# Two tables of sums for even and odd experts in the scatter of a mixture of experts

## The chip, the cores and the metric

One core of a Trainium2 chip. The metric is the time of one execution on the device, in microseconds (us). TensorE does the matmuls, VectorE and ScalarE the elementwise work, GpSimd (POOL in the profile) issues the indirect DMAs, SyncE (SP) the direct ones. All DMAs of the core run on its 16 DMA engines.

## The reference

An encoder layer for 1024 tokens of width 1024, in float32: a diagonal state space model and an attention beside each other, a projection with residual and layer norm, then a mixture of experts with a second layer norm. Only the last part matters here:

```python
scores = sigmoid(x1 @ w_router)                 # 64 experts
choice = scores + router_bias                   # top 4 of 8 groups, then top 6 experts
top_w  = top_w / top_w.sum() * 2.5              # weights of the 6 experts of a token
for each block of 128 tokens of one expert e:   # xb: [128, 1024]
    hb = silu(xb @ we_gate[e]) * (xb @ we_up[e])            # [128, 256]
    routed[tok] += (hb @ we_down[e]) * w[:, None]           # scatter with add
shared = (silu(x1 @ ws_gate) * (x1 @ ws_up)) @ ws_down
out = layer_norm(alpha * x1 + routed + shared)
```

## The kernel before, in words

The program has stages that follow each other: `project`, `attention`, `s5_scan`, `s5_gate`, `mix_norm_route` and `moe_experts`. Each has one instruction stream per engine, written out by hand, which wait for each other by semaphores. The change touches the last two.

**`mix_norm_route`** (to line 1388) computes x1 for eight tiles of 128 tokens, routes them, and writes into the DRAM table `slot_d` which token goes to which slot of which expert: VectorE computes the destinations (`route`, `place`), GpSimd scatters (line 1121). SyncE first loads small parameters, waits for `blank_done`, writes blanks over `slot_d` (line 1094), and then stores each finished tile of x1 into `x1_d` (line 1098). At the end the shared expert's gate and up run; ScalarE's `gate(n)` (line 1242) writes `sig` there, a tile of 128 x 1024.

**`moe_experts`** (from line 1391) begins with the shared expert's down product on TensorE (line 1583); VectorE adds alpha times x1 (line 1700), and SyncE stores the eight tiles as the start values of the DRAM table `sum_d` (line 1448). Then 65 blocks follow: one of 128 slots for each of the 64 experts, and one overflow block (more are skipped by tests on `n_over`). For block e:

- GpSimd copies the indices into `idx` (line 1489) and issues four indirect DMAs, a quarter of each row's columns each (line 1493), which gather 128 rows of x1 into `xg[e % 2]`. It waits for `x_turned`, so that the buffer is free.
- VectorE transposes `xg` into `xgT` (line 1678), TensorE computes `p_gu`, gate and up together (line 1547: eight calls of 128x512), ScalarE the sigmoid (line 1615), VectorE the products `gs` and `h` (lines 1683, 1685), TensorE turns h (line 1555), VectorE copies it to `hT`, TensorE computes `p_y` (line 1567, four calls of 128x512).
- ScalarE and VectorE scale one half of `p_y` each into `y[e % 2]` (`keep_y`, lines 1621 and 1695). They wait for the scatter two blocks back, which read the same buffer.
- GpSimd scatters `y` into `sum_d` with an add (line 1504). Before that it waits until the scatter of the block before has landed (line 1502), since two blocks can hold the same token and an add that is in flight reads the old value.

GpSimd's order is gather(e + 4), then scatter(e + 1), and so on; TensorE's is `gate_up(e + 1)`, `down(e)`, `turn_h(e + 1)`. The weights of an expert (three times 1 MB) lie in a ring of four buffers, one of them the tile `o` of the mixers. SyncE loads expert e (lines 1449 to 1454, 1011 and 1015) as soon as block e - 4 has finished its down product; experts 0 to 3 are loaded ahead of the loop, and the overflow block's expert by `load_over(0, 0)`.

When all is scattered, GpSimd has gone through its skipped overflow rounds (lines 1530 to 1535) and has waited for `y_out` (line 1536), SyncE reads the eight tiles of `sum_d` back (line 1476). For each tile t the second layer norm runs: ScalarE adds up the row (line 1663), VectorE makes the mean (`center`, line 1749), ScalarE squares (line 1652), VectorE makes the variance and subtracts the mean (`spread`, lines 1755 and 1756), ScalarE takes the root (line 1657), and VectorE finishes (`finish`, lines 1760 and 1761); SyncE stores the tile (line 1480). VectorE's order is center(t), finish(t - 1), spread(t). TensorE has nothing to do in this part.

## Time and profile before

| | |
|---|---|
| median of three runs | 1798.69 us (1796.7 to 1800.16) |
| profiled execution | 1799.06 us, its span 1797.2 us |
| TensorE matmul busy | 1565.6 us, 87% of the span |
| VectorE / ScalarE / GpSimd busy | 852.0 / 361.7 / 434.0 us |
| DMA | 317.26 MB, 177 GB/s over the span |
| granted TensorE clock, mean | 0.927 |
| expert blocks | first scatter at 1048.7 us, last at 1756.1 us |
| second layer norm | first read of `sum_d` at 1764.14 us |

The page gives busy times of each engine, the chain of work that ended last (followed back from the last instruction, at each step to what released it), the costliest groups of instructions, and for DMAs the time from issue to landing. Times in views are from the start of the span. A matmul call in float32 stands as two instructions. In a group, "idle before" is the time that the engine waited ahead of these instructions, with what ended the wait. Names are without buffer numbers: `sum_d<-moe_y,moe_idx` is the scatter, `moe_xg<-x_d,moe_idx` the gather, `all_x_sb` the tile `k.x`.

### The profile page before, as it was taken

What the parts mean: (1) busy time and instruction counts of PE and PEld (TensorE: products, weight loads), DVE (VectorE), ACT (ScalarE), POOL (GpSimd) and SP (SyncE); (2) the same over time, 40 slices, a digit from 0 to 9 for tenths busy, and PEclk for the clock granted to TensorE, in tenths of its full rate; (3) what the DMA queues carried; (4) which work ended last, traced back from release to release, by engine and by line L of the source; (5) the groups of instructions that cost most, each with busy time, mean ns of one, the idle gap of its engine ahead of it and who ended that gap; (6) DMA issues with size and microseconds to landing.
All of it is one profiled execution on the core that took longest, in us unless ns stands there. A gap on an engine that the chain in (4) does not pass through costs nothing. (4 is left out here: it accounts for less than half of the span.)

```text
span 1797.2 us, 18459 instructions
## 1 busy us (share of the span) xinstructions
PE 1565.6 (87%) x5878; PEld 893.5 (50%) x5878; DVE 852.0 (47%) x1618; ACT 361.7 (20%) x616; POOL 434.0 (24%) x444
## 2 busy tenths in 40 slices
PE   7988999999946555389999999999999999999990
PEld 4545777777735554335554444444444444444440
DVE  1462444444588888324886333333333333333335
ACT  1303444434333113111220010000000000000014
POOL 0000000000000000000234345555555555555530
PEclk9997999999967666689999999999999999999995
DMA  9010000000051101530005679999999999999965
GB/s 233 12 43 4 5 4 4 4 4 1 1 54 17 23 12 23 203 137 24 36 25 203 235 245 368 367 367 361 363 369 369 363 361 368 366 370 366 360 188 204
DMA packets 105149, 317.26 MB, mean 177 GB/s; under 512 B 38358, under 2 KB 55406, under 8 KB 80146
## 3 DMA queue, kind: packets, MB, share of 16 engines
q1 hardware_dynamic: 80546, 257.26, 38.8%
q0 software_dynamic: 23408, 59.45, 13.6%
q8 instruction: 23, 0.38, 0.1%
q10 hardware_dynamic: 1152, 0.00, 0.0%
q14 instruction: 20, 0.16, 0.0%
HBM read 271.73 MB, written 51.72 MB: 180 GB/s over the span
## 5 line engine op out<-in xcount | busy, mean ns | idle before, releaser
L1547 PE MATMUL moe_p_gu<-mixers_ring,moe_xgT 128*128 128x512 f32 x784 | 344.6, 592 | 0.0
L1678 DVE STREAM_TRANSPOSE moe_xgT<-moe_xg 128x1024 f32<-128x1024 f32 x65 | 132.0, 2031 | 423.8 <-DMA moe_xg<-x_d,moe_idx 423.8
L1493 POOL DMA_INDIRECT moe_xg<-x_d,moe_idx x260 | 264.3, 1017 | 116.1 <-issue 60.2
L1121 POOL DMA_INDIRECT slot_d<-all_entry,all_dest_i x48 | 48.1, 1003 | 926.8 <-DVE all_dest_i L1333 914.7
L1567 PE MATMUL moe_p_y<-mixers_ring,moe_hT 128*128 128x512 f32 x520 | 233.9, 592 | 0.9 <-DVE moe_hT L1689 0.9
L1547 PEld LDWEIGHTS moe_p_gu<-mixers_ring,moe_xgT 128*128 128x128 f32 x784 | 145.7, 191 | 164.5 <-issue 164.5
L1504 POOL DMA_INDIRECT sum_d<-moe_y,moe_idx x65 | 105.5, 1623 | 245.3 <-DMA sum_d<-moe_y,moe_idx 209.6
L1567 PEld LDWEIGHTS moe_p_y<-mixers_ring,moe_hT 128*128 128x128 f32 x520 | 98.7, 190 | 125.0 <-issue 123.9
L1615 ACT ACTIVATE moe_sig<-moe_p_gu 128x256 f32<-128x256 f32 x65 | 25.0, 384 | 585.0 <-PE moe_p_gu L1547 585.0
L582 PEld LDWEIGHTS att_p_o<-att_v,att_prT 128*128 128x128 f32 x1024 | 120.4, 192 | 19.5 <-issue 17.6
L582 PE MATMUL att_p_o<-att_v,att_prT 128*128 128x64 f32 x1024 | 123.7, 274 | 1.5 <-DVE att_prT L659 1.5
L529 PE MATMUL att_p_s<-latents_kT,att_qT 96*128 96x512 f32 x256 | 122.3, 601 | 0.0
L645 DVE TENSOR_REDUCE att_nmax<-att_p_s 128x1 f32<-128x1024 f32 x64 | 78.4, 1225 | 92.4 <-PE att_p_s L529 92.1
L1547 PE MATMUL moe_p_gu<-mixers_o,moe_xgT 128*128 128x512 f32 x256 | 113.9, 598 | 1.0
L752 PE MATMUL ssm_p_v<-ssm_U,ssm_w_in 128*128 x256 | 53.1, 397 | 45.3 <-DVE ssm_gsn L859 31.8
L1547 PEld LDWEIGHTS moe_p_gu<-mixers_o,moe_xgT 128*128 128x128 f32 x256 | 47.3, 190 | 57.2 <-issue 57.1
L752 PEld LDWEIGHTS ssm_p_v<-ssm_U,ssm_w_in 128*128 128x128 f32 x256 | 50.3, 303 | 49.5 <-DVE ssm_gsn L859 34.4
L615 ACT ACTIVATE att_pr<-att_p_s,att_bias 128x1024 f32<-128x1024 f32 x64 | 71.0, 1110 | 3.1 <-DVE att_bias L646 3.1
L568 PE MATMUL att_p_t<-all_const,att_pr 128*128 128x128 f32 x512 | 66.9, 274 | 0.9 <-ACT att_pr L615 0.9
L620 ACT ACTIVATE att_prT<-att_p_t 128x512 f32<-128x512 f32 x64 | 38.2, 597 | 138.5 <-PE att_p_t L568 138.5
L1621 ACT ACTIVATE moe_y<-moe_p_y,shared_block_w 128x512 f32<-128x512 f32 x65 | 44.7, 688 | 100.6 <-PE moe_p_y L1567 100.6
L1695 DVE TENSOR_SCALAR moe_y<-moe_p_y,shared_block_w 128x512 f32<-128x512 f32 x65 | 48.7, 749 | 27.7 <-PE moe_p_y L1567 27.1
(314 smaller groups left out, 1966.7 us busy)
## 6 DMA issues: line engine op xcount, KB each, us to landing
mixers_ring<-in_we_down_dram SPq DMA_DIRECT2D x65, 1024.0 KB, 17.3
mixers_ring<-in_we_gate_dram SPq DMA_DIRECT2D x49, 1024.0 KB, 7.7
mixers_ring<-in_we_up_dram SPq DMA_DIRECT2D x49, 1024.0 KB, 14.3
mixers_o<-in_we_gate_dram SPq DMA_DIRECT2D x16, 1024.0 KB, 8.0
mixers_o<-in_we_up_dram SPq DMA_DIRECT2D x16, 1024.0 KB, 14.7
moe_xg<-x_d,moe_idx POOLq DMA_INDIRECT x260, 6.8
all_x_sb<-in_x_dram SPq DMA_DIRECT2D x8, 512.0 KB, 12.3
mixers_ring<-in_w_o_dram SPq DMA_DIRECT2D x1, 4096.0 KB, 22.4
```

What stands on the lines that cost most here:

```text
L529: last = nc.tensor.matmul(p_s[:, t % 2, half * 512:(half + 1) * 512], qT[:, u, t * P:(t + 1) * P], kT[:, u, half * 512:(half + 1) * 512], ...
L568: last = nc.tensor.transpose(p_t[:, j, :], pr[:, t % 2, j * P:(j + 1) * P], k.ident)
L582: last = nc.tensor.matmul(p_o[:, 0:DV], prT[:, t % 2, j, :], v[:, u, j, :], start=(j == 0), stop=(j == T - 1))
L615: nc.scalar.activation(pr[:, t % 2, :], p_s[:, t % 2, :], ACT.Exp, bias=bias[:, t % 2:t % 2 + 1], scale=SCALE, accum_out=total[:, t % 4:t ...
L645: ch.link(nc.vector.tensor_reduce(nmax[:, t % 2:t % 2 + 1], p_s[:, t % 2, :], AX.X, ALU.max, negate=True))
L752: last = nc.tensor.matmul(p_v[:, x % 2, part, r, :], w_in[:, gd, part * N:part * N + P], U[:, bass.ds(b * GB + half * 4 + r, 1), :].rearra ...
L1493: nc.gpsimd.indirect_dma_start(xg[:, u, g, :], None, x1_quarters, bass.IndirectOffsetOnAxis(ap=idx[:, c, g:g + 1], axis=0), bounds_check=N ...
L1504: nc.gpsimd.indirect_dma_start(k.sum_d[:, :], bass.IndirectOffsetOnAxis(ap=idx[:, c, NQ:NQ + 1], axis=0), y[:, u, :], None, compute_op=ALU ...
L1547: last = nc.tensor.matmul(p_gu[:, u, :], xgT[:, u, kk, :], k.moe_gu[v][:, :, kk * F:(kk + 1) * F], start=(kk == 0), stop=(kk == KD - 1))
L1567: last = nc.tensor.matmul(p_y[:, half * 512:(half + 1) * 512], hT[:, u, kk, :], k.moe_dn[v][:, kk * D + half * 512:kk * D + (half + 1) * 512],
L1678: nc.vector.transpose(xgT[:, u].rearrange("p k (g i) -> p g k i", g=NQ), xg[:, u].rearrange("p g (j k) -> p g k j", k=KD)).then_inc(x_turn ...
L1695: nc.vector.tensor_scalar(y[:, u, 512:D], p_y[:, 512:D], k.block_w[:, bass.ds(col, 1)], None, ALU.mult).then_inc(y_dve, 1)
```

## The change

There are two DRAM tables of sums. Even blocks scatter into table 0, odd ones into table 1, and each table has a semaphore `y_out[u]` of its own. A scatter, and `keep_y`, wait for the scatter of the same parity before. Table 0 starts as before; table 1 is set to zero in `mix_norm_route` by one DMA from the tile `sig`, which VectorE wipes first; ScalarE's first `gate` waits for that DMA. At the end SyncE reads both tables, the second one into the ring's `gate_up` buffers 0 and 1, TensorE adds the two tiles by two matmuls with the identity matrix per half into PSUM (`p_sum`, two tiles that take turns), and the layer norm reads PSUM where it read `k.x`. GpSimd's loop has 9 rounds of six blocks instead of 10, the rest is written out; the order of its gathers and scatters is the same.

```diff
-    k.sum_d = nc.dram_tensor("sum_d", (SEQ + P, D), f32).ap()
+    k.sum_d = [nc.dram_tensor(f"sum{u}_d", (SEQ + P, D), f32).ap() for u in range(2)]
...
             sp.wait_ge(blank_done, 1)
+            sp.wait_ge(wiped, 1)
+            sp.dma_start(k.sum_d[1].rearrange("(b p) d -> p b d", p=P),
+                         sig[:, :, :].rearrange("p f t -> p (f t)").unsqueeze(1).to_broadcast([P, T + 1, D])).then_inc(wiped_d, 16)
...
             def gate(n):
                 act.wait_ge(gu_done, n + 1)
+                if n == 0:
+                    act.wait_ge(wiped_d, 16)
...
+            nc.vector.memset(sig[:, :, :], 0.0).then_inc(wiped, 1)
             tokens = k.tok.unsqueeze(2).to_broadcast([P, T, TOP_K])
...
+        part = [k.moe_gu[t // 4].rearrange("p h (a d) -> p (h a) d", d=D)[:, t % 4, :] for t in range(T)]
+        p_sum = [p_y[:, :], p_gu[:, :, :].rearrange("p u w -> p (u w)")]
-        y_out = sem("y_out")
+        y_out = [sem(f"y_out{u}") for u in range(2)]
...
-            sp.wait_ge(all_out, 1)
+            sp.wait_ge(all_out, 2)
             for t in range(T):
-                sp.dma_start(k.x[:, t, :], k.sum_d[t * P:(t + 1) * P, :]).then_inc(sum_in[t], 16)
+                sp.dma_start(k.x[:, t, :], k.sum_d[0][t * P:(t + 1) * P, :]).then_inc(sum_in[t], 16)
+                sp.dma_start(part[t], k.sum_d[1][t * P:(t + 1) * P, :]).then_inc(sum_in[t], 16)
...
-            def scatter(n, u, c, first=False):
+            def scatter(n, u, c, landed):
                 pool.wait_ge(y_act, n + 1)
                 pool.wait_ge(y_dve, n + 1)
-                if not first:
-                    pool.wait_ge(y_out, n * 16)
+                if landed is not None:
+                    pool.wait_ge(y_out[u], landed)
                 pool.sem_inc(y_taken, 1)
-                nc.gpsimd.indirect_dma_start(k.sum_d[:, :], bass.IndirectOffsetOnAxis(ap=idx[:, c, NQ:NQ + 1], axis=0),
-                                             y[:, u, :], None, compute_op=ALU.add).then_inc(y_out, 16)
+                nc.gpsimd.indirect_dma_start(k.sum_d[u], bass.IndirectOffsetOnAxis(ap=idx[:, c, NQ:NQ + 1], axis=0),
+                                             y[:, u, :], None, compute_op=ALU.add).then_inc(y_out[u], 16)
...
-            with pool.Fori(0, (E - 4) // 6) as ee:
+            gather(4, OVER + 4, 0, 4, free=3)
+            scatter(1, 1, 1, None)
+            LOOPED = (E - 5) // 6 * 6
+            with pool.Fori(0, LOOPED // 6) as ee:
                 for v in range(6):
-                    e = ee * 6 + v
-                    gather(e + 4, ee * 6 + (OVER + 4 + v), v % 2, (v + 4) % 6, free=e + 3)
-                    scatter(e + 1, (v + 1) % 2, (v + 1) % 6)
+                    gather(ee * 6 + (v + 5), ee * 6 + (OVER + 5 + v), (v + 1) % 2, (v + 5) % 6, free=ee * 6 + (v + 4))
+                    scatter(ee * 6 + (v + 2), v % 2, (v + 2) % 6, ee * 48 + (v // 2 + 1) * 16)
...
-            pool.wait_ge(y_out, n_over * 16 + 16 * E)
-            pool.sem_inc(all_out, 1)
+            for u in range(2):
+                pool.wait_ge(y_out[u], (n_over + (1 - u)) // 2 * 16 + 8 * E)
+                pool.sem_inc(all_out, 1)
...
+            for t in range(T):
+                pe.wait_ge(sum_in[t], 32)
+                if t >= 2:
+                    pe.wait_ge(squared, t - 1)
+                    pe.wait_ge(centered, t - 1)
+                for half in range(2):
+                    cols = slice(half * 512, (half + 1) * 512)
+                    nc.tensor.matmul(p_sum[t % 2][:, cols], k.ident, k.x[:, t, cols], start=True, stop=False)
+                    last = nc.tensor.matmul(p_sum[t % 2][:, cols], k.ident, part[t][:, cols], start=False, stop=True)
+                last.then_inc(summed, 1)
...
-                act.wait_ge(sum_in[t], 16)
+                act.wait_ge(summed, t + 1)
...
-                nc.scalar.activation(junk[:, :], k.x[:, t, :], ACT.Copy, accum_out=tot[:, 0, t:t + 1]).then_inc(added, 1)
+                nc.scalar.activation(junk[:, :], p_sum[t % 2], ACT.Copy, accum_out=tot[:, 0, t:t + 1]).then_inc(added, 1)
...
-                ch.link(nc.vector.scalar_tensor_tensor(k.x[:, t, :], k.x[:, t, :], nmean[:, t:t + 1], g2[:, :], ALU.add, ALU.mult))
+                nc.vector.scalar_tensor_tensor(k.x[:, t, :], p_sum[t % 2], nmean[:, t:t + 1], g2[:, :], ALU.add, ALU.mult).then_inc(centered, 1)
```

The square reads `p_sum` in the same way, and `keep_y` on both engines waits for `y_out[u]`.

## Rows read from the trace of the kernel before

**Rows 1.** The page, part 4: chain that ended last, shares of the span, by line.
```profile
DMA sum_d<-moe_y,moe_idx 34%; PE moe_p_s L1583 2%; PE moe_p_gu L1547 2%; PE moe_p_y L1567 1%; DVE all_x_sb L1761 1%; DMA moe_xg<-x_d,moe_idx 0%; DVE all_x_sb L1756 0%; DMA all_x_sb<-sum_d 0%; POOLq L1489 0%; POOL moe_xg L1493 0%; POOLq L1530 0%; POOL sum_d L1504 0%; ACT moe_junk L1663 0%; DVE moe_y L1695 0%; ACT L1657 0%
```

**Rows 2.** Line 1504, its instructions: ns min/median/max, first and last start; then its landings.
```profile
L1504 POOL DMA_INDIRECT sum_d<-moe_y,moe_idx x65: 1552/1626/1636, 1048.7 to 1756.1; - x65
...
DMA to landing us min/median/max: 6.3/10.3/11.4
```

**Rows 3.** Stretch 1600 to 1700: busy us of five engines, clock, DMA share, GB/s.
```profile
1600.00:1700.00 100.00, 97.22 (x235) 42.47 (x234) 33.73 (x46) 9.65 (x18) 52.19 (x55) 1.00 1.03 364
```

**Rows 4.** Timeline of TensorE, 1731 to 1748: start us, busy us.
```profile
1735.61 0.39 PE L1555 MATMUL moe_p_h<-all_const,moe_h 128*128 128x128 f32 x2
1735.84 7.03 PE L1547 MATMUL moe_p_gu<-mixers_ring,moe_xgT 128*128 128x512 f32 x16
...
1746.14 0.39 PE L1555 MATMUL moe_p_h<-all_const,moe_h 128*128 128x128 f32 x2
```

**Rows 5.** One microsecond of the expert loop, columns as in rows 3.
```profile
1404.00:1405.00 1.00, 1.00 (x3) 0.38 (x3) 0.00 (x0) 0.00 (x0) 0.00 (x0) 1.00 1.01 422
```

**Rows 6.** DMA issues in 1150:1172 and then in 1590:1612, last column us to landing.
```profile
mixers_ring<-in_we_down_dram SPq DMA_DIRECT2D x2, 1024.0 KB, 13.9
...
mixers_ring<-in_we_down_dram SPq DMA_DIRECT2D x2, 1024.0 KB, 18.8
```

**Rows 7.** Timeline of SyncE, first and last expert load of the loop.
```profile
1047.12 0.35 SPq L1011 DMA_DIRECT2D mixers_ring<-in_we_gate_dram  x1
...
1713.96 0.38 SPq L1011 DMA_DIRECT2D mixers_ring<-in_we_up_dram  x1
```

**Rows 8.** DMA issues in 1713:1715, the last loads, last column us to landing.
```profile
mixers_ring<-in_we_up_dram SPq DMA_DIRECT2D x1, 1024.0 KB, 15.7
mixers_ring<-in_we_down_dram SPq DMA_DIRECT2D x1, 1024.0 KB, 17.7
```

**Rows 9.** Timeline of GpSimd, 1404 to 1430; in brackets its idle time.
```profile
1416.77 1.62 POOL L1504 DMA_INDIRECT sum_d<-moe_y,moe_idx  x1 [3.44 <-DMA sum_d<-moe_y,moe_idx]
```

**Rows 10.** DMA queues in 1394:1417: packets, MB, share of 16 engines.
```profile
q0 software_dynamic: 687, 1.91, 32.9%
```

**Rows 11.** The chain in order of time, end of the expert loop: start us, us, what.
```profile
1747.13 0.72 issue
1747.86 7.40 DMA sum_d<-moe_y,moe_idx
...
1762.72 0.21 issue
...
1763.31 0.21 issue
...
1764.14 3.13 DMA all_x_sb<-sum_d
```

**Rows 12.** Timeline of all engines, 1736 to 1765.
```profile
1751.22 0.75 DVE L1695 TENSOR_SCALAR moe_y<-moe_p_y,shared_block_w 128x512 f32<-128x512 f32 x1 [3.79 <-PE moe_p_y L1567]
1756.12 1.55 POOL L1504 DMA_INDIRECT sum_d<-moe_y,moe_idx  x1 [6.70 <-DMA sum_d<-moe_y,moe_idx]
```

**Rows 13.** DMA busy tenths in 40 slices of 799 to 819.5.
```profile
DMA  8998999994100000000000100000000000000000
```

**Rows 14.** Timeline of VectorE, 1755 to 1797: the spreads of tiles 1 and 7.
```profile
1774.22 1.28 DVE L1756 SCALAR_TENSOR_TENSOR all_x_sb<-all_x_sb,moe_nmean,moe_g 128x1024 f32<-128x1024 f32 x1
...
1791.36 1.28 DVE L1756 SCALAR_TENSOR_TENSOR all_x_sb<-all_x_sb,moe_nmean,moe_g 128x1024 f32<-128x1024 f32 x1
```

**Rows 15.** DMA issues in 1764:1765, last column us to landing.
```profile
all_x_sb<-sum_d SPq DMA_DIRECT2D x2, 512.0 KB, 3.7
```

**Rows 16.** The microsecond from 1754, columns as in rows 3.
```profile
1754.00:1755.00 1.00, 0.00 (x0) 0.00 (x0) 0.00 (x0) 0.00 (x0) 0.00 (x0) 0.56 0.03 8
```

**Rows 17.** Line 1583 in 1000:1003: ns min/median/max, first to last start.
```profile
L1583 PE MATMUL moe_p_s<-shared_dn,shared_hT x4: 1002/1061/1061, 999.7 to 1002.2; 128*128 128x512 f32 x4
```

**Rows 18.** Groups of instructions in 1764:1797: busy us, mean ns.
```profile
L1663 ACT ACTIVATE moe_junk<-all_x_sb 128x1024 f32<-128x1024 f32 x8 | 8.5, 1059 | 17.8 <-DMA all_x_sb<-sum_d 17.1
```

More of the change, by code:

```diff
@@ L1447, in _ @@
                 sp.wait_ge(s_read, 2 * t + 2)
-                sp.dma_start(k.sum_d[t * P:(t + 1) * P, :], k.x[:, t, :]).then_inc(sum_out, 16)
+                sp.dma_start(k.sum_d[0][t * P:(t + 1) * P, :], k.x[:, t, :]).then_inc(sum_out, 16)
             with sp.Fori(1, E // RING) as ee:
@@ L1513, in _ @@
             pool.wait_ge(sum_out, 16 * T)
-            scatter(0, 0, 0, first=True)
-            with pool.Fori(0, (E - 4) // 6) as ee:
-                for v in range(6):
-                    e = ee * 6 + v
-                    gather(e + 4, ee * 6 + (OVER + 4 + v), v % 2, (v + 4) % 6, free=e + 3)
-                    scatter(e + 1, (v + 1) % 2, (v + 1) % 6)
-            gather(E, 0, 0, 4, free=E - 1)
-            scatter(E - 3, 1, 1)
-            scatter(E - 2, 0, 2)
-            scatter(E - 1, 1, 3)
-            scatter(E, 0, 4)
+            scatter(0, 0, 0, None)
+            gather(4, OVER + 4, 0, 4, free=3)
+            scatter(1, 1, 1, None)
+            LOOPED = (E - 5) // 6 * 6
+            with pool.Fori(0, LOOPED // 6) as ee:
+                for v in range(6):
+                    gather(ee * 6 + (v + 5), ee * 6 + (OVER + 5 + v), (v + 1) % 2, (v + 5) % 6, free=ee * 6 + (v + 4))
+                    scatter(ee * 6 + (v + 2), v % 2, (v + 2) % 6, ee * 48 + (v // 2 + 1) * 16)
+            for n in range(LOOPED + 5, E + 1):
+                gather(n, OVER + n if n < E else 0, n % 2, n % 6, free=n - 1)
+                scatter(n - 3, (n - 3) % 2, (n - 3) % 6, (n - 3) // 2 * 16)
+            for n in range(E - 2, E + 1):
+                scatter(n, n % 2, n % 6, n // 2 * 16)
             n_over = pool.value_load(k.n_over[0:1, 0:1], min_val=0, max_val=OVER)
@@ L1528, in _ @@
                     gather(E + j, j, j % 2, 4 + j % 2, free=E + j - 1)
-                    scatter(E + j, j % 2, 4 + j % 2)
+                    scatter(E + j, j % 2, 4 + j % 2, E * 8 + j // 2 * 16)
             with pool.Fori(1, OVER // 4) as round_, pool.If(n_over > round_ * 4):
@@ L1707, in _ @@
             hidden(1, 1)
-            keep_y(0, 0, OVER, sent=False)
+            keep_y(0, 0, OVER, None)
             keep_hT(1, 1)
```

50 lines of the change are left out of this document (26 added, 24 removed).

## The prediction

> **What bounds the kernel now.** I begin with the chain of work that ended last: 34% of the span is one DMA, the accumulating scatter into `sum_d` [rows 1]. Its line says more: 65 of them, from 1048.7 to 1756.1, with a median landing of 10.3 us, while the quickest took 6.3 [rows 2]. From the first to the last a step takes 707.4 / 64 = 11.05 us: one landing and some 0.75 us of GpSimd. That reads as if the expert loop were a string of scatters.
>
> A chain names what came last, not what would come next, so I look at the others. TensorE is busy 97 of 100 us [rows 3]; where nothing held it, one turn of `moe_p_h` follows the last after 1746.14 - 1735.61 = 10.53 us [rows 4]. It would allow 0.52 us less per expert.
>
> The DMA engines are the third. In a stretch of 100 us their busy share is 1.03 [rows 3], and in a single microsecond with 422 GB/s it is 1.01 [rows 5]: they are never free. The weights show the same. Down weights land 13.9 us after issue near 1150 and 18.8 near 1590 [rows 6], so a queue grows while loads are issued every 11 us. The loop loads 61 experts (4 to 64), the first from 1047.12; the last up load goes out at 1713.96, the down load 0.5 later and lands after 17.7, at 1732.1 [rows 7, 8]. That is 685 / 61 = 11.23 us per expert, slower than the beat of the scatters; the four buffers, full at the start, pay the difference. So DMA throughput bounds this loop, with the scatters' wait right behind it, and the landing of 10.3 us is long because the engines are full.
>
> **The change, part by part.** The sum is made against the profiled execution, 1799.06 us (span 1797.2), which is 0.37 above the median shown, 1798.69.
>
> *The wait in the loop.* Gathers keep their distance from scatters; a scatter now waits for `y` and the scatter two back. GpSimd sat 3.44 us idle before the scatter at 1416.77, for the landing of the one before [rows 9]. So scatters and the gathers behind them go some 3.4 us earlier, and with them VectorE's transposes and TensorE. What is late next are the weights. The last up weights were in at 1713.96 + 15.7 = 1729.7 [rows 7, 8]; TensorE began that `gate_up` at 1735.84 [rows 4]. The margin is 6.1 us, all that the loop can give if the bytes take the same time. Part of it goes: with scatters ahead, one scatter's packets that came after this landing now come before it. The indirect DMAs of about two experts held 32.9% of the engines for 23 us [rows 10], 3.8 us per expert, so the scatter's share is between 0 and 3.8; I take the middle, 1.9. Gain of the loop: 6.1 - 1.9 = 4.2 us. Its bounds: 0 (moved packets and a worse mix eat it) and 33.3, TensorE's own beat, 64 x (11.05 - 10.53). I stay near the low end because the share of 1.03 leaves no gap.
>
> The Trainium skill ("DMA: Bandwidth & Descriptors", Specifications) gives about 358 GB/s as one core's limit from HBM. By it the loop, at 364 GB/s in the stretch of rows 3, stands at the limit; the gain would be nothing and the total 4.2 us more. The microsecond at 422 GB/s [rows 5] doesn't keep to that figure, so the measurement decides.
>
> *The end of the loop.* The last half of `y` is finished at 1751.22 + 0.75 = 1751.97, but scatter 64 is issued at 1756.12, after scatter 63, issued at 1747.86, has landed 7.4 us later [rows 11, 12]. The time before, ready to issue took 0.72 us [rows 11]. Without the wait: 1752.7, a gain of 3.4 us. From there to SyncE's first read at 1764.14 are 8.0 us, in which GpSimd's sequencer skips the 11 empty rounds of lines 1530 to 1535, 1763.31 - 1762.72 = 0.59 us each [rows 11]; scatter 64's landing is hidden under them, now as before. The two new waits compute their values in registers: 0 to 0.6 us, I take 0.2, the lower end, since they are a few such steps.
>
> *The wipe of the second table.* SyncE issues 9 x 512 KB at about 798, ahead of the blanks and the `x1_d` stores. The DMA engines fall idle some 5 us later and stay so but for one small transfer [rows 13]; at 200 to 420 GB/s the wipe takes 11 to 24 us. The blanks are wanted when the first tile has been routed, `x1_d` by the first gather of the expert stage, ScalarE's added wait comes when the mixing is nearly done: all much later. The memset on VectorE comes before its first real work of the stage, which waits for TensorE's first products. Cost 0; if this cover went, 11 to 24 us.
>
> *The end.* Here the change adds work to the path. Before, a tile took (1791.36 - 1774.22) / 6 = 2.86 us, in the loop spread, center, square, spread [rows 14]. Three terms:
> - The first tile's second read. The first read lands after 3.13 us [rows 11], the median of the first two is 3.7 [rows 15], so the second needs about 4.2 from its own issue 0.45 later: +1.5 us. Later tiles need 1 MB per 4 us, well below 422 GB/s; SyncE's 16 issues and the stores behind the reads are covered too.
> - The first sum. A tile takes four f32 matmuls of 512 columns, and each is two instructions (`gate_up` has eight calls, and x16). At full clock 24 instructions take 1735.84 to 1746.14, 0.43 us each, 3.43 a tile [rows 4]. But the granted clock falls to 0.5, 1.2 GHz, in the microsecond from 1754, after TensorE stopped at about 1751 [rows 16]; the new sums start some 15 us after it stopped. At 1.2 GHz four starts lie (1002.2 - 999.7) / 3 = 0.83 us apart [rows 17], 6.7 a tile. There the full clock came back after about 4 us of matmuls, so I take 4 us at half and the rest at full: +5.6 us. Ends: 3.4 and 6.7.
> - The pace. `p_sum` has two halves, so the sum of tile t+2 waits for square and spread of t. The loop over two tiles is the 2.86 of before plus sum 3.43, its last columns 0.25, ScalarE's add 1.06 and its accumulator 0.2, and 0.25 for semaphores: 8.05, 4.02 a tile [rows 4, 14, 18]. Six steps x (4.02 - 2.86) = 7.0 us.
> Together 14.1. Ends: 11.9 with the first sum at full clock, about 36 with all at half (8.2, then 7 x (6.7 - 2.86)).
>
> **Sum:** -4.2 - 3.4 + 0.2 + 14.1 = +6.7, so 1805.8 against the profiled execution and 1805.4 against the median.
>
> **Rivals.**
> *Transfers aren't the bound.* If the share of 1.03 hides reserve, TensorE sets the beat of 10.53: -33.3 - 3.4 + 14.3 = -22.4, 1776.3. For it: the chain [rows 1] and TensorE's 97%. Against: growing landings, a share without a gap [rows 3, 5, 6]. To be faster at all the loop must give over 10.9 us, so the DMA time per expert must fall from 11.23 to below 11.12. Chance 0.09.
> *The two ends cancel.* The margin of 6.1 us is won whole, with up to 2 more from a steadier mix, and the sums run at full clock: -8 - 3.4 + 0.2 + 11.9 = +0.7, 1799.4. Chance 0.16, of which 0.03 ends beyond no change on the fast side.
> *The clock doesn't come back at the end.* TensorE waits once in two tiles there. Sums at about 5 us each cost 22 instead of 14.1: 1813.3; all at half 1827.3. Against: at half clock TensorE has hardly a pause. Chance 0.13.
> The Trainium skill ("TensorE: Matmul & The Clock Gate", HAM oscillation) describes a kernel whose waits between groups of matmuls throttled TensorE each time, which would be this rival. The fall at 1754 agrees with it.
> *The scatter's wait only moves.* Two accumulates in flight slow each other and the loop gives 0: 1809.6. That lies within the forecast's own range; with it the forecast holds 0.62.
>
> **How the numbers follow.** Likeliest 1805.4. A measurement can tell 0.2%, 3.6 us, from no change. Slower: 0.62 + 0.13 = 0.75. Same: 0.16 - 0.03 = 0.13. Faster: 0.09 + 0.03 = 0.12. The range, 1798 to 1817, takes in cancelling and a partly throttled end; left out are the fast rival and an end mostly at half clock.
>
> **What would show it.** Scatters issued without waiting for the one before; landings of down weights that climb past 19 us to 22 and more; TensorE waiting for weights late in the loop; the last `gate_up` about 4 us earlier; scatter 64 less than 1 us after `y`. At the end: matmuls of about 1.06 us first, then 0.59; spreads 4 us apart; some 47 us from the first read to the end against 33. I am wrong if the last weights land more than 3 us before 1732, or if the tiles at the end keep a pace of 3 us.

## The result, and the profile after

The changed kernel takes 1804.41 us (median of 11 runs, 1803.09 to 1806.47), the kernel before 1796.7 in the same session (11 runs, 1790.22 to 1802.43). The ratio is 1.0035, with a 95% interval of 1.0023 to 1.0047: slower by 0.35%, some 6 us. These two medians lie 7.7 us apart; over all sessions the kernel before had medians of 1796.7 to 1799.15, from which the changed kernel is 5.3 to 7.7 us away. The changed kernel's profiled execution took 1805.89 us, its span 1804.1.

**The loop.** In the page, part 4, the chain that ended last no longer runs through the scatter (34% of the span before, [rows 1]):

```profile
PE 26%; DMA 17%; DVE 1%; issue 1%; SPq 0%; ACT 0%; POOLq 0%; POOL 0%; DVEq 0%
PE moe_p_gu L1560 15%; DMA mixers_ring<-in_we_up_dram 10%; PE moe_p_y L1580 7%; DMA mixers_o<-in_we_up_dram 6%; PE moe_p_s L1596 2%; PE moe_p_gu L1630 0%; PE moe_p_gu L1631 0%; DVE all_x_sb L1785 0%; PE moe_p_h L1568 0%; SPq L1011 0%; DVE all_x_sb L1779 0%; DMA mixers_ring<-sum_d 0%; PE moe_p_y L1630 0%; PE moe_p_y L1631 0%; POOLq L1542 0%
```

Its DMA share now belongs to the up weights. The scatter's line says why (the instructions, then the idle time of GpSimd before them, us and times, by what ended it):

```profile
L1514 POOL DMA_INDIRECT sum_d<-moe_y,moe_idx x65: 1552/1625/1635, 1049.9 to 1748.8; - x65
...
  DVE moe_y L1718: 232.8, 64
  DMA sum_d<-moe_y,moe_idx: 3.6, 1
```

64 of the 65 scatters now wait for `y` alone. The stretches of the loop (busy us of PE, PEld, DVE, ACT, POOL, then granted clock, DMA share, GB/s):

```profile
1100.00:1200.00 100.00, 99.97 (x248) 45.55 (x248) 35.61 (x47) 9.63 (x18) 55.00 (x57) 1.00 1.03 366
1200.00:1300.00 100.00, 95.90 (x235) 43.34 (x234) 35.24 (x45) 9.63 (x18) 53.10 (x55) 1.00 1.03 368
1600.00:1700.00 100.00, 97.39 (x237) 44.09 (x236) 35.47 (x45) 9.63 (x18) 53.06 (x55) 1.00 1.03 365
```

TensorE reaches 99.97 of 100 us in the first (96.35 before the change), then falls back to 95.9 and 97.4, where it was before (97.2 in [rows 3]), at the same share of 1.03 and 365 to 368 GB/s. The chain in order of time (start us, us, what) shows what holds it then:

```profile
1609.89 22.63 DMA mixers_o<-in_we_up_dram
...
1632.57 7.13 PE moe_p_gu L1560 x16
...
1654.43 22.19 DMA mixers_o<-in_we_up_dram
...
1676.67 7.13 PE moe_p_gu L1560 x16
...
1698.56 22.54 DMA mixers_o<-in_we_up_dram
...
1721.24 7.10 PE moe_p_gu L1560 x16
```

A buffer is refilled as soon as TensorE frees it, the up weights need 22.5 us, and TensorE starts when they land. The issues in the chain lie (1698.56 - 1609.89) / 8 = 11.08 us per expert apart. So the beat (the time from one expert to the next) was 10.53 us while the buffers had a lead, to about 1196, some 15 experts. Over the last 48 experts it was (1731.85 - 1195.87) / 48 = 11.17 us, practically the 11.13 of the same experts before, for another reason. The median landing of the up loads (the time from issue to landing) went from 14.3 us to 21.8 where the page gives one (`e1_loop_only`, which has the same loop).

**The end.** Timeline of the changed kernel (start us, us, engine, line; in brackets the idle time before and what ended it):

```profile
1748.76 1.55 POOL L1514 DMA_INDIRECT sum_d<-moe_y,moe_idx  x1 [3.33 <-DVE moe_y L1718]
1755.69 0.34 SPq L1485 DMA_DIRECT2D all_x_sb<-sum_d  x1
...
1760.35 2.07 PE L1630 MATMUL moe_p_y<-all_x_sb,all_const 128*128 128x512 f32 x2 [13.16 <-DMA mixers_ring<-sum_d]
...
1765.62 1.02 PE L1631 MATMUL moe_p_y<-mixers_ring,all_const 128*128 128x512 f32 x2
...
1766.68 1.02 ACT L1686 ACTIVATE moe_junk<-moe_p_y 128x1024 f32<-128x1024 f32 x1 [20.48 <-PE moe_p_y L1631]
...
1770.11 1.02 ACT L1686 ACTIVATE moe_junk<-moe_p_gu 128x1024 f32<-128x1024 f32 x1 [0.83 <-PE moe_p_gu L1631]
...
1795.33 1.02 ACT L1686 ACTIVATE moe_junk<-moe_p_gu 128x1024 f32<-128x1024 f32 x1 [2.00 <-PE moe_p_gu L1631]
```

Scatter 64 leaves 0.78 us after `y` (1747.98), the reads start 8.45 us earlier than before (1764.14, [rows 11]), and then 48.4 us pass to the end of the span, where it was 33.1. The granted clock is low at the first sum (columns as above):

```profile
1752.00:1753.00 1.00, 0.00 (x0) 0.00 (x0) 0.00 (x0) 0.00 (x0) 0.00 (x0) 0.50 0.94 176
1764.00:1765.00 1.00, 1.00 (x3) 0.48 (x2) 0.00 (x0) 0.00 (x0) 0.00 (x0) 0.50 1.04 418
1765.00:1766.00 1.00, 1.00 (x2) 0.30 (x2) 0.00 (x0) 0.00 (x0) 0.00 (x0) 0.70 1.01 414
1766.00:1767.00 1.00, 1.00 (x4) 0.47 (x3) 0.00 (x0) 0.32 (x1) 0.00 (x0) 1.00 1.06 430
```

It was 0.5, 1.2 GHz, from about 1752, after TensorE had stopped at 1747, and is back at 1.00 in the microsecond from 1766. TensorE had taken up the sums at 1760.35.

The balance of the two profiled executions, in us:

| term | before | after | difference |
|---|---|---|---|
| SyncE's first expert load of the expert stage | 998.33 | 999.57 | +1.24 |
| from there to the last `gate_up` | 737.51 | 732.28 | -5.23 |
| from there to the first read of the table | 28.30 | 23.84 | -4.46 |
| from there to ScalarE's first add | 3.16 | 10.99 | +7.83 |
| from the first add to the eighth | 21.18 | 28.65 | +7.47 |
| from there to the end of the span | 8.72 | 8.77 | +0.05 |
| sum | 1797.2 | 1804.1 | +6.9 |

The first line is scatter among executions and not of the change: over the profiles of all kernels here it lies between 996.6 and 1000.0, and from the mix stage's first VectorE product to it the two executions differ by 0.01 us (190.81, 190.82).

### The profile page after: what moved, and what is told of

It is laid out like the page before. It is cut to its first block and busy times, and to the rows that moved or that the text cites. A ratio compares the mean times of both kernels' runs of the same rounds, so it can differ in the third digit from the quotient of the medians.

```text
span 1804.1 us, 18556 instructions
## 1 busy us (share of the span) xinstructions
PE 1591.7 (88%) x5942; PEld 912.8 (51%) x5942; DVE 858.9 (48%) x1619; ACT 360.7 (20%) x616; POOL 432.9 (24%) x444
## 5 line engine op out<-in xcount | busy, mean ns | idle before, releaser
L1560 PE MATMUL moe_p_gu<-mixers_ring,moe_xgT 128*128 128x512 f32 x784 | 347.3, 596 | 14.1 <-DMA mixers_ring<-in_we_up_dram 13.9
L1560 PEld LDWEIGHTS moe_p_gu<-mixers_ring,moe_xgT 128*128 128x128 f32 x784 | 145.2, 190 | 183.9 <-issue 177.7
## 6 DMA issues: line engine op xcount, KB each, us to landing
sum_d<-mix_s_sig SPq DMA_DIRECT2D x1, 4608.0 KB, 17.5
```

Of the source, the lines that this page charges most:

```text
L1560: last = nc.tensor.matmul(p_gu[:, u, :], xgT[:, u, kk, :], k.moe_gu[v][:, :, kk * F:(kk + 1) * F], start=(kk == 0), stop=(kk == KD - 1))
```

## The experiments

### One part at a time: loop alone, end alone

`e1_loop_only`: the two tables and the scatters of the change, but at the end only table 0 is read and normalized. The sums of the odd experts (table 1) and TensorE's additions are left out.

```diff
-                sp.dma_start(part[t], k.sum_d[1][t * P:(t + 1) * P, :]).then_inc(sum_in[t], 16)
-            for t in range(T):
-                pe.wait_ge(sum_in[t], 32)
...
-                act.wait_ge(summed, t + 1)
+                act.wait_ge(sum_in[t], 16)
```

> The changed kernel without its end: only table 0 is read back and the sums of odd experts are left out, no sum on TensorE, the layer norm reads the tile as before. My theory (the DMA engines bound the loop, the end stage costs the rest): the last gate and up product starts about 4 us earlier than in the kernel before, the first read of the sums 8 to 9 us earlier, the end stage is 33 us again, so 7 to 10 us faster than the kernel before, about 1788. Rival 1 (transfers are not the bound, the loop's gain is hidden by something at the end): over 20 us faster. Rival 2 (the loop gives nothing, only the last scatter does): 3 to 4 us faster.

`e2_tail_only`: every scatter goes to table 0 and waits for the one before it, as before the change; table 1 stays zero and is still read and added.

```diff
+                if landed is not None or u:
+                    pool.wait_ge(y_out[1 - u], 16 * u if landed is None else landed + 16 * u)
-                nc.gpsimd.indirect_dma_start(k.sum_d[u], ...
+                nc.gpsimd.indirect_dma_start(k.sum_d[0], ...
```

> The changed kernel with every scatter going into table 0 and waiting for the one before it, so the loop is that of the kernel before and the end stage the new one (table 1 stays zero, the result is complete). My theory: the loop's beat is 11.05 us and the first read of the sums at about 1764 as before, the end stage takes 48 us instead of 33, in all 14 to 16 us slower than the kernel before, about 1812. Rival (part of the 15 us comes from what the faster loop leaves behind, such as the clock or the stores): under 12 us slower.

Measured: `e1_loop_only` 1788.27 us, ratio 0.9943 (0.9929 to 0.9957); `e2_tail_only` 1815.65 us, ratio 1.009 (1.0075 to 1.0105); the kernel before beside both 1798.99. That is -10.7 and +16.7 us. The first is as expected, the second a little above its 14 to 16. Together they make +6.0, which is the change: the parts add, within the 4 us or so that the two intervals leave. The chain of `e2_tail_only` shows the old wait at its place:

```profile
1750.18 6.93 DMA sum_d<-moe_y,moe_idx
...
1766.60 0.34 SPq L1485
...
1766.99 4.13 DMA mixers_ring<-sum_d
```

while in that of `e1_loop_only` the reads start at 1753.35 and ScalarE at 1756.53:

```profile
1753.35 3.17 DMA all_x_sb<-sum_d
...
1756.53 1.16 ACT moe_junk L1675 x2
```

Its span ends 33.05 us after the first read, as before the change.

### The wipe alone

`e9_wipe_only`: the kernel before, with only a second table that nothing uses, the memset of its zeros, the 4.5 MB transfer and one wait for it.

```diff
+            sp.wait_ge(wiped, 1)
+            sp.dma_start(k.sum1_d.rearrange("(b p) d -> p b d", p=P), ...).then_inc(wiped_d, 16)
...
+                if n == 0:
+                    act.wait_ge(wiped_d, 16)
```

> The kernel before with one thing added: the 4.5 MB of a second table that nothing uses are filled with zeros at the place where the changed kernel does it (about 800 us, on SyncE's queue), with one wait for it ahead of the first scatter. Theory of the prediction: the wipe costs nothing, since between the first VectorE product of the mix stage and the start of the expert stage the two profiles show 190.82 and 190.81 us: the kernel before's own time within 0.1%, ratio 0.999 to 1.001. Rival: the expert stage started 1.2 us later in the changed kernel's profile, and that is the wipe's: ratio 1.0005 to 1.0012, with the expert stage starting 1 to 2 us later.

Measured: 1799.37 us beside 1798.76, ratio 1.0001 (0.999 to 1.0012). Its expert stage started at 996.56, the earliest of all profiles. The wipe costs nothing that can be told from 0 within 2 us, and with it in place a stage can start earlier than in any other profile, so nothing ties the later start in the changed kernel's profile to it.

### Is it the transfers that hold the loop?

`e5_before_less_dma` and `e6_after_less_dma`: the kernel before and the changed one, each with only half of every expert's down weights loaded (512 KB instead of 1 MB). The other half of each buffer is not refilled; the matmuls are the same in number and size.

```diff
-    eng.dma_start(k.moe_dn[slot][:, :], k.we_down[0]....then_inc(k.dn_in[slot], 16)
+    eng.dma_start(k.moe_dn[slot][:, 0:D], k.we_down[0]...[bass.ds(expert, 1), :, 0:D]....then_inc(k.dn_in[slot], 16)
```

> The kernel before with half of each expert's down weights left out of the load (the other half keeps old data), 0.5 MB of 3 MB less per expert; products and scatters are all done. My theory (the DMA engines bound the loop, and the scatter's landing of 10.3 us is long only because they are full): the DMA time per expert falls by about 1.3 us to 9.9, the landing of a scatter to 9 us or less, and the beat goes from 11.05 to TensorE's 10.53 to 10.65 although every scatter still waits for the one before; 25 to 33 us faster than the kernel before. Rival (the scatter's wait is a bound of its own): the landing stays near 10.3 and the beat at 11.0, under 5 us faster.

> The changed kernel with the same half of the down weights left out. My theory: TensorE sets the beat all through the loop, 10.53 us, no waits for up weights; the loop ends about 29 us earlier than in the changed kernel, about 1776. Against the kernel before with the same cut it is slower by 10 to 12 us, since the wait was worth little once transfers are short and the end stage still costs 15 us. Rival (the scatter's wait is a bound of its own): it is over 10 us faster than the kernel before with the cut.

Measured: 1764.24 us for before (ratio 0.9806, 0.9789 to 0.9823) and 1773.62 for the change (0.9863, 0.9848 to 0.9878). Half a megabyte less per expert is worth 35 us to a kernel whose chain named the scatter alone; 25 to 33 were expected. The second kernel is 9.4 us slower than the first, where 10 to 12 were expected. The stretch of 500 us in each, `e5_before_less_dma` first (columns as above):

```profile
1200.00:1700.00 500.00, 498.78 (x1230) 226.59 (x1229) 184.59 (x238) 51.19 (x96) 276.17 (x281) 1.00 1.01 330
```

```profile
1200.00:1700.00 500.00, 500.00 (x1237) 228.10 (x1236) 186.52 (x238) 51.36 (x96) 275.21 (x280) 1.00 1.01 330
```

Both keep TensorE's beat of 10.53 us, with the scatter waiting for the one before it in the first and not in the second. The last `gate_up` comes 702.7 us after the stage's first load in one and 701.6 in the other: without the transfers' limit the two-table scatter is worth 1.2 us in the loop, by one trace each, not 5 or 6. The changed kernel and `e6_after_less_dma` both scatter without that wait, and between them the beat goes from 11.17 to 10.53 us by shorter transfers alone.

One expectation was missed: the median landing of a scatter in `e5_before_less_dma` is 9.7 us and not 9 or less, against 10.3 in the kernel before [rows 2]. With 0.75 us of GpSimd 9.7 fits into 10.53, and 10.3 did not. GpSimd still sat idle for scatters for 177.7 us (209.6 before); the wait remained, but it cost TensorE almost nothing.

The stretches also show what the DMA share can't tell. It is 1.01 here too, at 330 GB/s, in two loops that TensorE holds. What sets them apart from a loop that transfers hold is that the landings don't grow: down weights land 11.6 us after issue near 1150 and 12.3 near 1590, where it was 13.9 and 18.8 [rows 6]:

```profile
mixers_ring<-in_we_down_dram SPq DMA_DIRECT2D x2, 512.0 KB, 11.6
...
mixers_ring<-in_we_down_dram SPq DMA_DIRECT2D x2, 512.0 KB, 12.3
```

### The end: who adds, and with how many buffers

`e3_gpsimd_sum`: GpSimd adds the two tables in SBUF, TensorE and PSUM stay out of it.

```diff
+            for t in range(T):
+                pool.wait_ge(sum_in[t], 32)
+                nc.gpsimd.tensor_tensor(k.x[:, t, :], k.x[:, t, :], part[t], ALU.add).then_inc(summed, 1)
```

> The changed kernel with the two tables added by GpSimd in place (one tensor_tensor of 128x1024 per tile), the layer norm reads the tile in SBUF as before. If the pace of the end stage comes from the sum on TensorE and from its two PSUM halves, the pace goes back to 2.86 us a tile, the first tile comes 1.5 us (second read) and one GpSimd add (1 to 2.5 us) later, so the end stage takes 36 to 37 us and the kernel is 4 to 7 us faster than before. Rival (the two reads per tile set the pace, 1 MB a tile, or GpSimd and VectorE disturb each other at the memory): a pace of 3.3 us or more and no gain over the kernel before.

Measured: 1803.68 us, ratio 1.0028 (1.0018 to 1.0038), no better than the change. The groups of the end stage (busy us, mean ns, then idle us before):

```profile
L1553 POOL TENSOR_TENSOR all_x_sb<-all_x_sb,mixers_ring 128x1024 f32<-128x1024 f32 x8 | 24.2, 3048 | 12.5 <-DMA mixers_ring<-sum_d 12.5
L1772 DVE SCALAR_TENSOR_TENSOR all_x_sb<-all_x_sb,moe_nmean,moe_g 128x1024 f32<-128x1024 f32 x8 | 17.9, 2238 | 0.0
L1778 DVE SCALAR_TENSOR_TENSOR all_x_sb<-all_x_sb,moe_rstd,moe_b 128x1024 f32<-128x1024 f32 x8 | 13.9, 1732 | 0.3
```

VectorE's two operations took 1276 and 1285 ns before the change and take 2238 and 1732 here. In the chain most take 3.0 to 3.2 us while GpSimd is adding, and 1.19 to 1.28 after it has ended. GpSimd's first addition, alone, took 2.33 us; the mean of the eight is 3.05. The two slow each other while both work on SBUF; what they share there was not tried by itself. The reads have a part too: the second tile's second read landed 7.85 us after its issue, and GpSimd sat idle 2.36 us for it. The rival that was named beforehand, a slower pace and no gain, is what came: 32.61 us from ScalarE's first add to its eighth, 4.66 a tile. The Trainium skill ("GPSIMD Engine Reference", Specifications) says that GpSimd's way to SBUF is shared with VectorE, with contention where a VectorE instruction runs in a two-port mode or has two inputs in SBUF. The trace agrees: both VectorE operations here have two.

`e4_third_psum`: the changed kernel with three PSUM buffers for the sums instead of two.

```diff
-        p_sum = [p_y[:, :], p_gu[:, :, :].rearrange("p u w -> p (u w)")]
+        p_sum = [p_y[:, :], p_gu[:, :, :].rearrange("p u w -> p (u w)"), p_s[:, :, :].rearrange("p u w -> p (u w)")]
-                if t >= 2:
-                    pe.wait_ge(squared, t - 1)
-                    pe.wait_ge(centered, t - 1)
+                if t >= 3:
+                    pe.wait_ge(squared, t - 2)
+                    pe.wait_ge(centered, t - 2)
```

> The changed kernel with three PSUM buffers for the sums instead of two (the shared expert's p_s is free by then), so the sum of tile t+3 waits for tile t. My theory of the pace (a loop over two tiles of 8.05 us through the two halves): TensorE alone sets it then, 3.43 us a tile, 6 x 0.57 = 3 to 4 us faster than the changed kernel, about 1801. Rival (TensorE or the reads set the pace, not the halves): no difference.

Measured: 1799.25 us, ratio 1.0005 (0.9996 to 1.0014), 5.2 less than the change. ScalarE's first and eighth adds in its timeline:

```profile
1765.68 1.02 ACT L1686 ACTIVATE moe_junk<-moe_p_y 128x1024 f32<-128x1024 f32 x1 [20.45 <-PE moe_p_y L1631]
...
1789.72 1.02 ACT L1686 ACTIVATE moe_junk<-moe_p_gu 128x1024 f32<-128x1024 f32 x1 [0.89 <-PE moe_p_gu L1631]
```

From the one to the other are 24.04 us for seven tiles, 3.43 each: TensorE's own time for one sum. With two buffers it was 28.65, 4.09 each. With the third the change costs nothing on balance, and gains nothing (the interval allows 0.7 us less to 2.5 us more).

### The end: clock, and an early read

`e8_warm_clock`: the changed kernel, with five matmul calls ahead of the sums whose result nothing reads.

```diff
+            for i in range(5):
+                nc.tensor.matmul(p_s[:, i % 2, :], k.ident, k.const[:, 0:512], start=True, stop=True)
             for t in range(T):
                 pe.wait_ge(sum_in[t], 32)
```

> The changed kernel with five unused matmuls of 512 columns (ten instructions) on TensorE ahead of the first sum, after its skipped rounds. If the clock costs what the trace of the changed kernel shows (6.1 us for the first sum against 3.4), the first sum runs at full clock and the kernel is 2 to 2.7 us faster than the changed one, about 1802. Rival (the matmuls come too early or too late to have an effect, or the first sum waits behind them): no difference or 1 to 2 us slower.

Measured: 1801.79 us, ratio 1.002 (1.0009 to 1.003), 2.6 less than the change. Timeline, the calls and ScalarE's first add:

```profile
1753.76 6.77 PE L1624 MATMUL moe_p_s<-all_const 128*128 128x512 f32 x10 [6.70 <-issue]
...
1764.01 1.02 ACT L1688 ACTIVATE moe_junk<-moe_p_y 128x1024 f32<-128x1024 f32 x1 [17.94 <-PE moe_p_y L1633]
```

From the first read (1755.56) to that add are 8.45 us instead of 10.99. The calls took up the half-clocked time while the tables were still under way. This measures the low clock's share of the change, about 2.5 us, as expected.

`e7_early_table`: three PSUM buffers; SyncE reads three tiles of table 1 as soon as its last scatter has landed, without waiting for table 0's; TensorE puts them into PSUM first.

```diff
+            sp.wait_ge(y_out[1], n_over // 2 * 16 + 8 * E)
+            for t in range(3):
+                read_part(t)
+            sp.wait_ge(y_out[0], (n_over + 1) // 2 * 16 + 8 * E)
...
+            for t in range(3):
+                add_table(t, True)
+            for t in range(T):
+                add_table(t, False)
+                if 1 <= t <= T - 3:
+                    add_table(t + 2, True)
```

> The changed kernel with three PSUM buffers, three tiles of table 1 read as soon as the last odd scatter has landed and put into PSUM by TensorE ahead of table 0, and SyncE waiting for the scatters itself instead of for GpSimd's rounds. My theory: the first sum is ready 1.7 us of matmuls after the first tile of table 0 has landed, about 6 us earlier than in the changed kernel; then TensorE's 3.43 us a tile; the end about 1791 to 1794, 5 to 8 us faster than the kernel before. Rival (the early reads delay the last scatter, or the clock is low again by then): a gain under 2 us over the kernel with three PSUM buffers, 1797 to 1799.

Measured: 1803.48 us, ratio 1.0024 (1.0014 to 1.0034). This misses the theory by 10 us and the rival too: it is 4 us slower than `e4_third_psum`, which has the third buffer alone. The first reads do go out earlier, at 1750.92, but TensorE works in order:

```profile
1755.44 3.75 PE L1640 MATMUL moe_p_s<-mixers_ring,all_const 128*128 128x512 f32 x4 [9.23 <-DMA mixers_ring<-sum_d]
...
1764.42 1.02 ACT L1704 ACTIVATE moe_junk<-moe_p_s 128x1024 f32<-128x1024 f32 x1 [19.20 <-PE moe_p_s L1640]
...
1768.62 3.00 PE L1640 MATMUL moe_p_s<-mixers_ring,all_const 128*128 128x512 f32 x4 [2.52 <-DVE all_x_sb L1797]
...
1771.41 2.58 PE L1640 MATMUL moe_p_y<-all_x_sb,all_const 128*128 128x512 f32 x4
...
1774.03 1.02 ACT L1704 ACTIVATE moe_junk<-moe_p_y 128x1024 f32<-128x1024 f32 x1 [3.19 <-PE moe_p_y L1640]
```

The table-0 half of tile 2 (1771.41) stood in TensorE's queue behind the table-1 half of tile 3, which waited for VectorE to centre tile 0 (1768.62, 2.52 us idle). Four instructions from 1755.44 ran at half clock, 3.75 us instead of 1.88. After the wait the clock fell once more, to 0.85 in the two microseconds from 1768 and to 0.50 in the next two: 3.00 and 2.58 us. From the first add to the eighth are 28.19 us, the pace of two buffers, in spite of three.

`e10_early_fixed` was to mend both faults of `e7_early_table`. Table 1's half stands directly ahead of table 0's from tile 2 on, and nine unread calls come first. `e11_third_warm`: `e4_third_psum` with the same nine calls.

```diff
+            for i in range(9):
+                nc.tensor.matmul(p_sum[2][:, 0:512], k.ident, k.const[:, 0:512], start=True, stop=True)
```

> The changed kernel with table 1 read early, as in e7_early_table, but TensorE's order is different: part 0, part 1, table 0 of tiles 0 and 1, and from tile 2 on both tables of a tile one after the other, in three PSUM buffers; nine products that nothing reads run before them, as in e8_warm_clock. Theory: e7 gained little because TensorE works in order and the table-0 half of tile 2 stood behind the part of tile 3, which waits for VectorE to centre tile 0, and because the clock was at half speed for the first 3.5 us. With both gone the first tile is ready for ScalarE at about 1760.5 instead of 1766.7, and the pace is TensorE's own 3.44 us a tile: 1791 to 1795, ratio 0.996 to 0.9985, which beats the kernel before too. Rival: the end goes by something else (the pace stays at 4 us a tile, or the reads issued early land late beside the last scatter): 1797 to 1801.

> The changed kernel with both single edits, three PSUM buffers and nine products that nothing reads ahead of the sums. Theory: the two gains are of different terms (the pace of the later tiles, the length of the first sum) and add: 1804.4 less 5.2 less 2.6 = 1796.6, between 1795.5 and 1798, ratio 0.9985 to 1.0. Rival: the sums' pace and the first sum hide one another, so that the better one alone counts: 1798.5 to 1800.

Measured: `e10_early_fixed` 1801.51 us, ratio 1.0015 (1.0005 to 1.0024); `e11_third_warm` 1800.23, ratio 1.0014 (1.0006 to 1.0023), 1 us more than `e4_third_psum`. Both miss the theory and lie just beyond the rivals' upper edges (1801 and 1800), but not for the rivals' reasons: nine calls at this place were too many. Timelines, first of `e10_early_fixed`, then of `e11_third_warm`:

```profile
1753.78 10.69 PE L1646 MATMUL moe_p_y<-all_const 128*128 128x512 f32 x18 [6.90 <-issue]
...
1764.30 1.88 PE L1640 MATMUL moe_p_s<-mixers_ring,all_const 128*128 128x512 f32 x4
```

```profile
1751.83 10.36 PE L1624 MATMUL moe_p_s<-all_const 128*128 128x512 f32 x18 [6.69 <-issue]
...
1762.02 1.02 PE L1632 MATMUL moe_p_y<-all_x_sb,all_const 128*128 128x512 f32 x2
```

TensorE's sequencer reached them only after its skipped overflow rounds, 6.7 us after the last expert; the clock had fallen by then and stayed at half for the first 5.5 and 4.8 us of them, and they held the real sums back: in `e11_third_warm` the first sum started 8.4 us after the first read, in `e4_third_psum` 5.2. The pace behind them was as foreseen (22.31 and 24.03 us from the first add to the eighth). So what failed was the place and number of the calls; `e4_third_psum` with five of them was not tried.

`e12_clock_kept`: the kernel of `e10_early_fixed` (early read, three buffers, its order of the halves), but instead of the nine calls one call ahead of each skipped round, and one behind them.

```diff
+            def spin():
+                nc.tensor.matmul(p_s[:, 0, :], k.ident, k.const[:, 0:512], start=True, stop=True)
             for j in range(1, RING):
+                spin()
                 with pe.If(n_over > j):
...
-            with pe.Fori(1, OVER // RING) as round_, pe.If(n_over > round_ * RING):
+            with pe.Fori(1, OVER // RING) as round_:
+                spin()
+                with pe.If(n_over > round_ * RING):
```

> The kernel of e10_early_fixed, but the products that nothing reads stand between TensorE's skipped overflow rounds (1747 to 1754 us, 6.7 us in which it does no work), one of them ahead of each round or group of rounds, and only one is left behind them. Theory: e10's nine products began at 1753.8 us, took 10.7 us because the first half of them ran at half clock, and held the first real product until 1764.3, though table 1's first tile had landed by about 1755. With the engine kept at work through the skipped rounds the granted clock stays at 1.0 and the first real product starts at about 1755.4; the 32 products' stretch of 27.5 us and the 8.9 us behind the last of them give an end near 1792: 1791 to 1795 by the device time, ratio 0.9965 to 0.9985, faster than both kernels. Rival: the clock falls all the same, since one product in a microsecond is too little, so that the first tiles run at half clock: 1796 to 1799, ratio 0.999 to 1.0. A third way: the products between the rounds lengthen the skipping itself, and the sums start late: 1799 and more.

Measured: 1796.59 us (11 runs, 1794.89 to 1798.24) beside 1799.13, ratio 0.9987 (0.9978 to 0.9997). It is the one kernel here that does the whole computation and beats both, by 0.13% over the kernel before, and the interval's end comes close to no difference. Its timeline and two stretches:

```profile
1745.43 12.18 PE L1624 MATMUL moe_p_s<-all_const 128*128 128x512 f32 x28
...
1758.31 1.88 PE L1646 MATMUL moe_p_s<-mixers_ring,all_const 128*128 128x512 f32 x4
...
1763.66 1.02 ACT L1715 ACTIVATE moe_junk<-moe_p_s 128x1024 f32<-128x1024 f32 x1 [19.05 <-PE moe_p_s L1646]
...
1785.97 1.02 ACT L1715 ACTIVATE moe_junk<-moe_p_gu 128x1024 f32<-128x1024 f32 x1 [0.89 <-PE moe_p_gu L1646]
```

```profile
1750.00:1752.00 2.00, 2.00 (x6) 0.89 (x5) 0.00 (x0) 0.00 (x0) 0.00 (x0) 1.00 0.84 184
1752.00:1754.00 2.00, 2.00 (x6) 0.82 (x5) 0.00 (x0) 0.00 (x0) 0.00 (x0) 1.00 1.05 301
```

The clock stays at 1.0, the first add comes at 1763.66 and the eighth 22.31 us later, 3.2 a tile. The result misses the expected 1791 to 1795 by 1.6 us. It lies in the range of the first rival, but that rival's reason, a falling clock, did not come. What came is the third way, in part: there are 14 rounds, and with a call ahead of each the skipping took 12.2 us instead of 6.7. The calls last to 1757.5, while table 1's first tile, read from 1748.55, had landed by about 1755 (the quickest of those reads took 6.2 us). TensorE was busy all through those 12 us, so the trace doesn't say how few calls would have kept the clock up. Fewer were not tried.

## Why the prediction was right

Predicted 1805.4, measured 1804.41; the range and the side held. By its steps:

- **The loop's bound.** Right. Removing the scatter's wait gave a loop held by the up weights, with landings of 22 us and more, at 11.17 us per expert, where 11.23 had been read from the loads. `e6_after_less_dma` brings that loop down to 10.53 by shorter transfers, and `e5_before_less_dma` the loop of before. The rival "transfers aren't the bound" falls with both. One reason that was given for it doesn't hold: the share of 1.03 "without a gap" says little, since it is 1.01 where TensorE is the bound. The growing landings were the good reason. The sign that was named for being wrong stayed out: in `e1_loop_only` the last down weights went out at 1707.35 and landed 24.0 us later, at 1731.4. Counted from the stage's first load, the last weights land 733.8 to 734.6 us later in the three kernels whose scatters wait for the one before, and 732.2 to 734.9 in the seven others whose traces give the landing. The stream of weights kept its length, and only what stood behind it became shorter.
- **The loop's gain.** Predicted -4.2. The stage's first load to the last `gate_up` takes 737.5 to 738.2 us in the three kernels whose scatters wait for the one before (`before`, `e2_tail_only`, `e9_wipe_only`), and 730.3 to 732.9, mean 731.8, in the nine of full transfers whose scatters do not: -6.0. The term was undersized by 1.8 us. The step that failed is "part of it goes": the margin of 6.1 us was won whole, the 1.9 for a scatter's packets moved ahead was not lost. The two profiled executions tell where the gain lies: counted from the stage's first load, after the first 15 experts at 10.53 us the changed kernel is 7.0 us ahead, and at the last `gate_up` 5.2. It is not spread over the loop.
- **The end of the loop.** Predicted -3.4 and +0.2. The balance gives -4.46, and `e6_after_less_dma` against `e5_before_less_dma` gives -4.46 too (23.84 against 28.30). Scatter 64 is out 0.78 us after `y` instead of 4.15, -3.37 as predicted. The remaining 1.1 us are behind it: 6.93 us from that scatter to the first read instead of 8.02, though the two new waits are in them. GpSimd's skipped rounds became shorter: a step of its chain repeats every 0.43 us there, where it took 0.59 [rows 11]. The prediction had them unchanged. Why they are shorter was not tried; the index terms in them were rewritten.
- **The wipe.** Predicted 0; `e9_wipe_only` measured 0.0001 of the time, with an interval that still allows 2 us. The transfer took 17.5 us, inside the 11 to 24 foreseen.
- **The end stage.** Predicted +14.1, measured +15.35 in the traces and 16.7 in the times of `e2_tail_only` (interval 13.5 to 18.9). Second read +1.5: the second read landed 4.23 us after an issue 0.39 later, +1.5. First sum 5.6: it took 6.3 us (1760.35 to ScalarE's start at 1766.68), since the full clock was not back before 1765, 5 us into the sums. The 4 us had been taken from the matmuls of [rows 17], which were not quite the same case: they began at 998.37 at full clock, which fell in the microsecond from 999, was 0.50 from 1000, and was back in the one from 1003. Pace +7.0: +7.47. The sum counted six steps, and from the first add to the eighth there are seven; a step cost 1.07 us more and not 1.16. A pair of tiles takes 7.98 us in the chain (1775.66, 1783.64), predicted 8.05. One sum of the prediction is off: 8.2 + 7 x (6.7 - 2.86) is 35.1 and not about 36, so its 1827.3 should be 1826.4, which changes neither range nor chance.
- **The clock rival.** It did not come: from 1766 to the last sum the clock was 1.00, with waits of 0.8 to 1.1 us once in two tiles. The Trainium skill ("TensorE: Matmul & The Clock Gate", HAM oscillation) describes a kernel that waits for a DMA after every short group of matmuls and is throttled by each of these waits. The change's trace shows no such fall at waits of 0.8 to 1.1 us, which are shorter than those of that kernel. In `e7_early_table` TensorE waited 2.5 us, and there the clock did fall once more within the sums, so that four instructions from 1768.62 took 3.00 us.
- **The two ends cancel.** Its first half came true in the main (the whole margin of the loop, but not the 2 us more), its second did not (the first sum was half-clocked).
- **The wait only moves.** It did not: the loop gained all of its margin. But two accumulates were hardly ever in flight together. In `e1_loop_only`, which has the same loop, a scatter landed after 10.4 us in the median (10.3 before), and the next one is issued 10.5 us after it early in the loop and 11.2 us later on, in the mean. Only scatter 64 starts well before the one ahead of it has landed, 4.89 us after it. There 63 landed after 7.5 us and 64 after 6.0, where it was 7.4 and 6.6 one after the other: no slowing is seen in this one pair, and under full load none of the runs tries it.

In the two profiled executions 1.0 us (loop) and 1.3 us (end of the loop) of gain more than forecast stood against 1.25 us of cost more and a start that came 1.2 us later. So the mechanism was right, but that the total came out at +6.9 where +6.7 was forecast is luck: four deviations of 1.0 to 1.3 us cancelled.

## What to carry to other kernels

A chain of waits names what came last, not what comes next: here it gave the scatter 34% of the span, and taking its wait away won 6 us of 33, because weights stood right behind it. Read the next limit, with its margin, before you pay for removing the first, and ask if the removal pays only until the buffers' lead is gone. A DMA share of 1.0 doesn't tell that transfers are the limit; landings that grow through the loop do. What is put on the exposed end of a kernel costs its full time there. TensorE came to this stage with a low clock, and had two buffers to work with: these two cost some 7 of the 15 us (2.5 by `e8_warm_clock`, 4.6 of the pace by `e4_third_psum`). `e12_clock_kept` avoids both, at the price of calls that begin the sums later than the reads would allow.

## What the runs showed of the hardware

- GpSimd and VectorE slow each other on f32 tiles of 128x1024 in SBUF: GpSimd's addition 2.33 us alone and 3.05 in the mean, VectorE's operation 1.28 alone and mostly 3.0 to 3.3 us beside it (`e3_gpsimd_sum`).
- The granted clock fell to 0.5 between 2 and 5 us after TensorE stopped: from 1752 in the changed kernel, which had stopped at 1747, from 1754 in the kernel before (stopped at 1751), from 1749 in `e10_early_fixed` (stopped at 1746.9). With matmuls running again without a gap it was back at 1.00 after 3.7 us (`e7_early_table`) to 5.5 us (`e10_early_fixed`), in the changed kernel after 5.2.
- It can fall when TensorE is already at work again: after a pause of 2.5 us it was 0.50 in the two microseconds from 1770 of `e7_early_table`, in which TensorE was busy throughout.
- One call of 0.86 us ahead of each skipped round, 14 in 12.2 us, kept TensorE busy and the clock at 1.0 (`e12_clock_kept`).
- Skipped rounds take time: 6.7 us on TensorE (14 of them), 7 us on GpSimd. In the changed kernel GpSimd's are on the path between the last expert and the end. TensorE's are not, since it then waits for the reads until 1760.35; they decide when unread calls ahead of the sums can begin.
- The engines' busy share doesn't tell how much they move: 1.01 at 330 GB/s (`e5_before_less_dma`) and 1.03 at 365 to 368 GB/s (the changed kernel).
